# One decoder layer on one core: kept down weights loaded earlier, matrix products between the first transposes, first loads reordered

## The reference

```
h   = rms_norm(x, norm1_g)
prj = h @ w_in                          # 1024 x 2856, split in 13 parts
x  += concat(nsa(prj), gla(prj)) @ w_out
h2  = rms_norm(x, norm2_g)
x  += moe(h2)                           # top 4 of 32 experts

def expert(xb, e):                      # w_gate_up[e] 1024 x 2048, w_down[e] 1024 x 1024
    hgu = xb @ w_gate_up[e] + b_gate_up[e]
    return clamped_swiglu(hgu) @ w_down[e] + b_down[e]
```

## Time and profile before

| | |
|---|---|
| median of 3 runs | 1060.52 us (1058.54 to 1060.62) |
| span of the profiled execution | 1056.8 us, the only time that is given for it |
| PE busy | 1015.2 us, 96% of the span |
| DVE, ACT, POOL busy | 311.4, 167.2, 15.8 us |
| DMA | 426.37 MB, mean 403 GB/s |
| chain that ended last | PE 66%, DMA 30%, DVE 2% |

### The profile page before, as it was taken

How to read it: one execution, slowest core, us unless ns; L and a number is a source line. 1 busy time by engine, 2 the same in 40 slices (tenths; PEclk the granted TensorE clock), 3 DMA queues, 4 the chain that set the end, 5 groups by cost and what they waited for, 6 DMA issues and landing times.

```text
span 1056.8 us, 12109 instructions
## 1 busy us (share of the span) xinstructions
PE 1015.2 (96%) x4965; PEld 409.4 (39%) x4965; DVE 311.4 (29%) x711; ACT 167.2 (16%) x324; POOL 15.8 (1%) x42
## 2 busy tenths in 40 slices
PE   9999999999999999999999999999999999999998
PEld 6555654333333333333233333333333333333333
DVE  1666675222212222222222222222112221222222
ACT  2433422111101111111011001111111110111111
POOL 4100000000000000000000000000000000000000
PEclk9999999999999999999999999999999999999999
DMA  9992599999999999999999999999999999999997
GB/s 293 361 381 85 215 368 378 419 426 432 431 430 429 433 433 426 433 433 433 432 429 433 434 432 429 432 434 432 429 434 433 430 429 431 431 432 429 422 424 288
DMA packets 37187, 426.37 MB, mean 403 GB/s; under 512 B 3927, under 2 KB 12207, under 8 KB 20513
## 3 DMA queue, kind: packets, MB, share of 16 engines
q1 hardware_dynamic: 35120, 424.52, 95.8%
q0 software_dynamic: 704, 1.04, 0.5%
q10 hardware_dynamic: 1328, 0.33, 0.1%
HBM read 424.83 MB, written 1.05 MB: 403 GB/s over the span
## 4 chain that ended last, share of the span: by engine, by line
PE 66%; DMA 30%; DVE 2%; issue 1%; ACT 0%; SPq 0%; DVEq 0%
PE bank L1859 26%; DMA pair<-in_w_down 26%; PE bank L1871 15%; PE bank L1426 5%; DMA pair<-in_w_gate_up 4%; PE bank L1893 4%; PE bank L1835 3%; PE bank L1701 2%; PE bank L1885 2%; PE bank L1843 1%; PE bank L1878 1%; PE bank L1498 1%; PE bank L2095 1%; PE bank L1458 1%; PE bank L1485 1%; PE bank L1468 1%
## 5 line engine op out<-in xcount | busy, mean ns | idle before, releaser
L1859 PE MATMUL bank<-pair,xs 128*64 128x512 f32 x2032 | 446.3, 594 | 20.3 <-DMA pair<-in_w_gate_up 19.2
L1859 PEld LDWEIGHTS bank<-pair,xs 128*64 128x64 f32 x2032 | 142.2, 137 | 319.1 <-issue 286.0
L1871 PE MATMUL bank<-pair,sig 128*64 128x512 f32 x960 | 212.4, 594 | 13.3 <-DMA pair<-in_w_down 13.3
L1319 DVE COPY gu<-bank 128x512 f32<-128x512 f32 x32 | 36.3, 1134 | 413.9 <-PE bank L1859 413.9
L1871 PEld LDWEIGHTS bank<-pair,sig 128*64 128x64 f32 x960 | 72.4, 137 | 149.1 <-issue 143.7
L794 ACT COPY gu<-bank 128x512 f32<-128x512 f32 x32 | 36.2, 1133 | 457.7 <-PE bank L1859 457.7
L903 DVE TENSOR_TENSOR xs<-bank,gt 128x512 f32<-128x512 f32 x31 | 21.4, 691 | 220.5 <-PE bank L1843 220.5
L1426 PE MATMUL bank<-stage,xt 128*128 128x512 f32 x160 | 72.2, 598 | 0.0
L1893 PE MATMUL bank<-ys,pgt 64*128 64x512 f32 x248 | 61.6, 615 | 0.0
L1835 PE MATMUL bank<-xr,onehot 128*64 128x512 f32 x248 | 58.5, 592 | 0.0
L799 ACT COPY ys<-bank 128x512 f32<-128x512 f32 x31 | 18.1, 585 | 206.4 <-PE bank L1871 206.4
(11 more groups left out here) (338 smaller groups left out, 524.9 us busy)
## 6 DMA issues: line engine op xcount, KB each, us to landing
pair<-in_w_gate_up SPq DMA_DIRECT2D x51, 4096.0 KB, 40.9
pair<-in_w_down SPq DMA_DIRECT2D x24, 4096.0 KB, 38.9
pair<-in_w_gate_up SPq DMA_DIRECT2D x20, 2048.0 KB, 12.8
pair<-in_w_down SPq DMA_DIRECT2D x18, 1024.0 KB, 12.2
stage<-in_w_in SPq DMA_DIRECT2D x5, 2048.0 KB, 19.0
pair<-in_w_down SPq DMA_DIRECT2D x4, 2048.0 KB, 31.0
pair<-in_w_gate_up SPq DMA_DIRECT2D x8, 1024.0 KB, 7.6
stage<-in_w_out SPq DMA_DIRECT2D x2, 2048.0 KB, 13.4
```

Of the source, the lines that this page charges most:

```text
L1319: V.tensor_copy(gu[:, 1, :].rearrange("p (i q) -> p q i", i=FQ), up_banks[1][:].rearrange("p (q i) -> p q i", i=FQ)).then_inc(s["gu_lo"], 1)
L1859: last = mm(up_banks[a][b * CAP:(b + 1) * CAP, :].rearrange("p (q i) -> p q i", i=FQ), xs[:, k, :], cols[:, b], start=k == 0, stop=k == DK ...
L1871: last = mm(down_bank[b * CAP:(b + 1) * CAP, :], actf[:, kk % FQ, kk // FQ, :], row[:, 512 * b:512 * (b + 1)], start=kk == 0, stop=kk == D ...
```

## The change

Four things change.

1. The two halves of `extra2` are issued much earlier: behind the first 2 MB of the ring's pair 0, ahead of front_used(5). In front of them SP waits for `tables` 2, `gsg` 1 and `qr_full` 3, the last readers of what `extra2` lies over. The temporaries move: `sgr` to the place of `xt`, `gsq` to that of `glrt` and `w2`, `s3` behind `gu`; the table `glag` moves too. As `xt` lies in slot 7, the load of pair 2's second half waits for `grg` as well (DVE's L1152).
2. PE's ten transposes of the identity are replaced by six products of a zeroed tile `warm` (DVE sets it), and one product of 64 columns is put after every second transpose and after every eighth.
3. `grows` is turned ahead of x, with two products behind it.
4. On ACT's queue the 64 KB load is issued ahead of `grows`. It shares `w_low` now, and `w_low` covers two row groups; the next two are told by `w_mid`.

```diff
+            def idle_product(n=P):
+                mm(banks[7][:, 0:n], warm[:], warm[:, 0:n], start=True, stop=True)
+
+            pe.wait_ge(s["dve"], 1)
+            for n in range(6):
+                idle_product()
             pe.wait_ge(s["const"], 2)
-            for n in range(10):
-                tp(banks[7][:, 0:P], ident[:], ident[:])
+            pe.wait_ge(s["grows1"], 16)
+            tp(banks[4][:, 0:DK], grows[:], ident[0:DK, 0:DK]).then_inc(s["g1_full"], 1)
+            idle_product()
+            idle_product()
             for ti in range(NT):
                 pe.wait_ge(s[f"xin{ti}"], 16)
                 for half in range(2):
                     for k in range(4):
                         c = 4 * half + k
                         last = tp(banks[2 * ti + half][:, k * P:(k + 1) * P], xr[:, ti, c * P:(c + 1) * P], ident[:])
+                        if k == 1:
+                            idle_product(CAP)
                     last.then_inc(s["xt_full"], 1)
-                if ti == 0:
-                    pe.wait_ge(s["grows1"], 16)
-                    tp(banks[4][:, 0:DK], grows[:], ident[0:DK, 0:DK]).then_inc(s["g1_full"], 1)
+                    idle_product(CAP)
...
-            pe.wait_ge(s["glrw"], 16)
             pe.wait_ge(s["g1t"], 1)
...
-                    pe.wait_ge(s["w_low"], 16)
+                    pe.wait_ge(s["w_low"], 32)
...
+                        if (half, ti, k) == (0, 0, 2):
+                            pe.wait_ge(s["w_mid"], 16)
...
+            act.dma_start(front_slot(0)[:, :, 280:280 + RANK], split_k(w_in[0])[:, :, GLR_AT:GLR_AT + RANK])\
+                .then_inc(s["w_low"], 16)
             act.dma_start(grows[:], norm1_g[0].rearrange("(k p) -> k p", p=P)).then_inc(s["grows1"], 16)
-            act.dma_start(front_slot(0)[:, :, 280:280 + RANK], split_k(w_in[0])[:, :, GLR_AT:GLR_AT + RANK])\
-                .then_inc(s["glrw"], 16)
...
-                    sp.dma_start(dst[:, 0:4, :], src[:, 0:4, :]).then_inc(s["w_low"], 16)
+                    sp.dma_start(dst[:, 0:2, :], src[:, 0:2, :]).then_inc(s["w_low"], 16)
+                    sp.dma_start(dst[:, 2:4, :], src[:, 2:4, :]).then_inc(s["w_mid"], 16)
...
             columns_in_place(0, 2, 0, 0, FF, "part0")
+            sp.wait_ge(s["tables"], 2)
+            sp.wait_ge(s["gsg"], 1)
+            sp.wait_ge(s["qr_full"], 3)
+            for half in range(2):
+                kept_half(extra2, KEPT[1], half)
             front_used(sp, 5)
...
             sp.wait_ge(s["o_full"], 1)
+            sp.wait_ge(s["grg"], 1)
             rows_in_place(2, 1, 0, 2, 4, "ring2")
...
             sp.dma_start(gu[:].rearrange("p a n -> p (a n)"), source(0, 0)[:, 0:FF]).then_inc(s["stage1"], 16)
-            for half in range(2):
-                kept_half(extra2, KEPT[1], half)
             product_done(sp, 5)
...
-        sgr = at("sgr", [P, NT, 512], F32, shared)
+        sgr = at("sgr", [P, NT, 512], F32, xt_at)
-        gsq = at("gsq", [P, 2, 512], F32, shared + 4096)
+        gsq = at("gsq", [P, 2, 512], F32, moe_at)
-        s3 = at("s3", [P, 4, P], F32, shared)
+        s3 = at("s3", [P, 4, P], F32, gu_at + 2048)
...
+            link(V.memset(warm[:], 0.0))
             dve.wait_ge(s["g1_full"], 1)
```

More of the change, by code:

```diff
@@ L130, in decoder_layer @@
         place[0] = spare[1]
+        xt_at = place[0]
         xt = sb("xt", [P, DK, S])
@@ L179, in decoder_layer @@
         grows2 = sb("grows2", [UP_PIECES, UP_K * P])
-        glag = sb("glag", [P, DV])
         wgate = sb("wgate", [RANK + 1, 256])
@@ L210, in decoder_layer @@
         ones = at("ones", [P, P], F32, late_at + 4 * 720)
+        glag = at("glag", [P, DV], F32, late_at + 4 * (720 + P))
         gtt = at("gtt", [P, S], F32, extra_at)
@@ L230, in decoder_layer @@
         qd, kd = eb, en
-        s3 = at("s3", [P, 4, P], F32, shared)
+        s3 = at("s3", [P, 4, P], F32, gu_at + 2048)
         s4 = at("s4", [P, 4, P], F32, moe_at + 2048)
         t1 = at("t1", [P, 4, 512], F32, extra_at)
+        warm = at("warm", [P, P], F32, a_at)
         s1 = at("s1", [P, 4, P], F32, b_at + 4096)
@@ L266, in decoder_layer @@
         s = {n: ctx.enter_context(nc.semaphore("s_" + n)) for n in (
-            "xin0 xin1 w_low grows1 grows g1_full g1t xt_full xt ms_x rsx proj_full proj small const act dve rope sin "
-            "late rows_full tables glrw glrt_full glrt decay_full absz loga bexp dec qd qdt_full qdt at_full ats "
+            "xin0 xin1 w_low w_mid grows1 grows g1_full g1t xt_full xt ms_x rsx proj_full proj small const act dve rope sin "
+            "late rows_full tables glrt_full glrt decay_full absz loga bexp dec qd qdt_full qdt at_full ats "
             "u_full sta sgr grg o_full gsq glaout kx_full kx post_full post tb h_full sigh hid ht_full hidt "
```

## The result

The change makes the kernel slower by a little: 1061.78 us, the median of 20 runs (1059.66 to 1063.93), against 1059.09 us, the median of 20 runs of the kernel before on the same chip (1057.43 to 1060.89). The ratio is 1.0022 (95% interval 1.0015 to 1.003), which is 2.3 us; the medians by themselves are 2.7 apart. The forecast was a gain of 2.4 us, the rival "the front gets longer" is what happened. The profiled span went from 1056.8 to 1060.8 us.

The account below looks back on a forecast made before the run. PE bounds the chain to about 450 us, then the expert-weight stream, whose start PE releases. Front 2.35 plus stream 0.1 gives 2.45 us off 1060.5: 1058.1 us, own range 1057.0 to 1059.3, 8 in 10 1055.2 to 1062.5.

Parts of the forecast that it names:

- the front gets longer: Rival, chance 0.20: PE stands behind a late `grows`, perhaps with the clock left low; run at 1063 to 1065 us.
- the front's unknown: Start of the kernel: when `grows` lands, being behind the 64 KB on ACT's queue and ahead of x on PE.
- Lower bound: ACT's queue at the start: the 64 KB's pieces go in beside x in 0.9 us, `grows` there at about 3.3.
- The upper bound: ACT's queue at the start: the 64 KB's pieces come only when x is through, `grows` at 5.5 to 7.4 us.
- I take it that the clock has risen by the time x is turned: Front: after six products ending at 3.6 us, PE runs at full clock when x's turning starts at 4.5 us.
- A half costs 0.87 + 3 x 0.107 = 1.2 us: Front: turning each half of x with its added products takes PE 1.2 us, ending at 5.7 and 7.1 us.
- the gain of 2.35: Front: the first projection ends at 15.3 instead of 17.66 us, and the gain of 2.35 us reaches the end.
- it rose only behind products: Front: PE's clock was read as rising behind products, not transposes, so swapping them in brings the rise forward.
- The 2 MB: Moved from 136.97 to behind 59.07 us: hidden in standing DMA time, leaving a hole; gain 0.1, bounded by 0 and 4.9 us.
- The three waits of SP: Waits for `tables`, `gsg`, `qr_full` ahead of the early 2 MB: told by about 60 us, SP comes at 62.3; cost 0.
- the price given for the case without slack: SP's added wait for `grg`, until 127.34 against an issue at 127.12: cost 0, or 0.3 us without slack.
- It is the issue that starts the continuous stream: At 156.74 us the backlog is just gone, so this issue, released by PE's product 4, starts the continuous weight stream.

Follow-up runs that it names:

- e3: Changed kernel with ACT's two loads swapped back, `grows` ahead of the 64 KB; ratio to the kernel before 1.0005 (0.9997 to 1.0014).
- e4: Changed kernel with `grows` turned behind the first half of x again, ACT's new load order kept; ratio to the kernel before 1.0008 (0.9999 to 1.0017).
- e1: Kernel before with only the early kept 2 MB, SP's added waits and the moved temporaries, old front; ratio 1.0005 (0.9996 to 1.0013).
- e7: Kernel before with four products of 512 columns added on PE ahead of the second projection; ratio 1.003 (1.0018 to 1.0042).
- e8: Kernel before with four products of 512 columns added on PE in expert step 3, at 234.5 us; ratio 1.0 (0.9991 to 1.0009).
- e11: Kernel before with the kept 2 MB issued behind the last load ahead of the experts, at 160.0 us; ratio 1.0014 (1.0005 to 1.0023).
- e12: Kernel before with the kept 2 MB issued further on, at 222.3 us; ratio 1.0054 (1.004 to 1.0067).
- e2: Kernel before with all of the new front, the kept 2 MB staying late; ratio 1.003 (1.0019 to 1.0042).
- e5: Changed kernel with the kept 2 MB issued behind `ring4`, at 163.6 us; ratio to the kernel before 1.0052 (1.0036 to 1.0067).
- e6: Kernel before with only the front's loads changed: 64 KB ahead of `grows`, `w_low` split; 1057.85 us, ratio 0.9992 (0.9983 to 1.0001).
- e10: Changed kernel with ten instead of six products at the start, filling PE's wait for `grows`; ratio to the kernel before 1.0018 (1.0007 to 1.0028).
- e13: Kernel before with only the front's loads changed, the same kernel as e6 on another chip; 1057.21 us, ratio 0.9986 (0.9977 to 0.9995).

## Why the prediction was wrong

**The failed step** is the front's unknown: "Lower bound: the 1024 pieces now issued at 0.82 go in beside x as `grows` did", and the choice made there, "I take the early one, since the issue at 0.82 is the row nearest to an issue at 0.82". `grows` landed at 5.70 us, not at 3.3 to 4. The row chosen was that of a load with 16 packets. The 64 KB's pieces, issued at the same time, did go in beside x, and about as fast as reckoned (994 in 0.8 us, where the forecast had 1024 in 0.9); what the bound left out is that they began only after 3 us, and that `grows` stood behind them in the queue. The upper bound (5.5) came near in its number but not in its reason, "only when x is through": nearly all were moved by 4.2 us, and the second half of x was there only at 6.2. What pointed the right way in the rows of before was a 64 KB load issued at 1.47 and without a packet up to 4.8.

**What hung on it**: "I take it that the clock has risen by the time x is turned". With a gap of 1.78 us ahead of it, it had not. From the forecast 15.3 to the measured 19.53 the sum goes: x starts at 7.02 instead of 4.5 (+2.5); turning takes 4.32 us, to 11.34, instead of 2.6 (+1.7); 0.3 of spare time ahead of L1515 is used (-0.3); L1515 takes 8.19 instead of 7.9 (+0.3). That is 4.2 us. The rival had this as one mechanism: with `grows` at 5.5 and the clock low "the end is 20 instead of 17.66", priced at 2.3 to 2.5 us on the run; measured are 19.53 and a ratio worth 2.3 us. e3 and e4, which take the wait away, bring the loss back to 0.0005 and 0.0008.

**A term mis-sized**: "A half costs 0.87 + 3 x 0.107 = 1.2 us". The trace has four products to a half, of two instructions each, and a pair with its product takes 0.40: 1.6 us. The products ahead of x were too cheap as well: the six end at 4.07 and not at 3.6, and the two behind `grows` take 1.0 us in e3 and not 0.43, as the clock is still low. Even with `grows` in time x is turned at 8.47 (e3), not at 7.1, and the gain of 2.35 would have shrunk to 1.0 against the profile of before.

**The base of that gain was too high as well.** Six profiles have ten transposes and the loads of before (before, e1, e7, e8, e11, e12): the first projection ends at 17.66, 16.23, 16.30, 16.62, 17.16 and 16.42, a mean of 16.73. The one on which the prediction rests is the latest of them. So e3 and e4 (16.66 and 16.35) gain nothing, and the changed kernel's one profile loses 2.8 us against the mean; e2 and e5, with the same front, end at 20.69 and 20.80. The median that the forecast was taken off, 1060.5 from three runs, was also 1.4 us above the 1059.09 of twenty. The prediction took the clock's late rise for a rule, "it rose only behind products", and leaned on the Trainium skill, TensorE: Matmul & The Clock Gate, Part 4 (PE-mode transpose), by which transposes do not engage the full clock. Here the measurements differ from the page: in e1 the second eight transposes take 1.09 us, in e6 the same, with nothing but transposes before them. The rise is early or late from profile to profile with transposes ahead, and was early (by 5.9 us) in all three profiles with products ahead and no gap, e3, e4 and e10.

**The 2 MB**: right. The forecast was 0.1 us, the burst's hole and the standing time are where it said, and e1 measures 1.0005 (0.9996 to 1.0013). The three waits of SP cost nothing that shows, and `grg` moved an issue to 129.30 us where 127.12 + 1.87 = 128.99 was due: 0.3, the price given for the case without slack, and lost in slack.

**Where the stream starts**: the place was wrong, the consequence right. "It is the issue that starts the continuous stream" at 156.74 does not hold: then 2 MB at 160 us would cost 4.9, and e11 costs 1.5 us (e5 against e2: 0.45 in the profile, 2.3 in time). The stream still has room up to 176 us (336 GB/s), and at 222 us the whole price is due (e12). Between these no place was tried. That PE's delay in the front arrives whole at the end is nevertheless true: e7, 3.2 for 3.4 us. In the changed kernel 1.87 at 19.53 us stands beside 2.68 at 894 us. Two profiles whose first projections end within 0.12 us of each other (e1 and e4) differ by 0.84 there, so I make nothing of the 0.8 between.

**The weight of the page on queues.** The Trainium skill, DMA: Bandwidth & Descriptors (Queues, rings and completion order), says that an engine goes round its queues by packets, and I let it speak for an early `grows`. Where both queues move, the trace agrees: from 3 to 4.8 us q10 moved 1038 packets and q1 140. But none of q10's 1024 pieces moved before 3 us, while q1 moved 73 packets, and the trace does not show whether the queue had any ready by then. So the page could not tell when the load begins, and that was the question.

## What to carry to other kernels

A tiny load that PE waits for first must be issued first on its queue; a load of 1024 small pieces ahead of it, 64 KB in all, put it off from 4.00 us or sooner (e3) to 5.70. Before PE time is added to raise the clock, look whether a wait still lies behind it, since the clock rose late in all three profiles with such a gap, and read the stage's end in more than one profile before calling a late rise the rule. What is won in a prologue is worth as much as the next thing that is late there: e12's early clock went into a wait for 64 KB, and only e6 and e13, with that load moved forward and the block's load divided, are faster than before.

## What the runs showed of the hardware beyond that

The moment at which the clock rises differs between profiles of the same front: the pace doubled at 10.8, 5.0, 5.1, 6.2, 9.9 and 5.2 us in the six profiles named above, at 6.4 and 10.3 in two of one and the same kernel (e6, e13). With six products, a gap for `grows` and more work it was 9.5, 11.9 and 12.2 us (after, e2, e5), late in three of three.

The clock can also fall in mid-kernel. In e2, e5 and e10 the trace has a stretch of 3.4 us at half clock that starts at 165.5, 165.8 and 162.9 us, in or behind the router, where the chain runs through many short steps of DVE and ACT. PE itself stands little there (0.14 us between 163 and 165 in e2, 0.22 between 161 and 163 in e10), and no less in the kernel before, which has no such stretch (0.21 between 161 and 163). The stretches of e2 (163 to 166.5 and 166.5 to 170 us; the clock is the third number from the end):

```profile
163.00:166.50 3.50, 3.28 (x21) 2.17 (x22) 1.73 (x11) 0.29 (x2) 0.00 (x0) 0.85 1.00 417
166.50:170.00 3.50, 3.50 (x14) 1.21 (x13) 2.13 (x10) 0.37 (x1) 0.00 (x0) 0.66 0.68 286
```

Both stretches read 1.00 in the kernel before. Four of e10's eleven runs have a mean clock of 0.997 or 0.998 and a median of 1062.5 us, the seven others one of 1059.2; with such a fall in some runs and not in others the front's own price can't be read to better than a microsecond from all runs of e2 and e10 together. The kernel before has them too, 8 of its 33 runs on e2's chip (a mean clock of 0.998 or less, a median of 1059.5 us against 1058.0). What brings it on was not tried.
